# Which heads share an attention step, and on which half of the matmul array each score lands

## The reference, cut to what matters

```
# 8 query heads of 64, in 2 key groups of 4; a chunk is 64 tokens, the window is 2 chunks
scores = einsum('bnqhgd,bnkhd->bnhgqk', q, k) * 64 ** -0.5
scores = scores - slope[head] * |distance|           # ALiBi, one slope per head
probs  = softmax([scores, sink[head]])[..., :-1]      # one sink logit per head
out    = einsum('bnhgqk,bnkhd->bnqhgd', probs, v)     # heads of a group share k and v
```

## Time and profile before

| | |
|---|---|
| median of the runs | 683.0 us (682.1 to 683.81) |
| the profiled execution: its own time | 682.08 us |
| the profiled execution: span from first to last instruction | 680.4 us |
| PE busy | 652.1 us, 96% of the span |
| DVE busy | 477.3 us, 70% |
| ACT busy | 397.7 us, 58% |
| mean granted TensorE clock | 0.99 of full speed |
| PE's share of the chain that ended last | 86% |

### The profile page before, as it was taken

One profiled execution on the slowest core, in us unless ns is written; L12 is line 12 of the kernel. 1 busy time (PEld: TensorE's weight loads), 2 busy tenths in 40 slices (PEclk: granted clock), 3 DMA queues, 4 the chain that ended last, 5 costly groups with the idle time before them and its releaser, 6 DMA issues.

```text
span 680.4 us, 9400 instructions
## 1 busy us (share of the span) xinstructions
PE 652.1 (96%) x3421; PEld 543.7 (80%) x3421; DVE 477.3 (70%) x801; ACT 397.7 (58%) x675; POOL 170.6 (25%) x217
## 2 busy tenths in 40 slices
PE   5999999999999999999999998889999999999985
PEld 4788878788888888888888886778888888888763
DVE  5788995264632435424674637999999999998877
ACT  7448584255633332334452356277898889898853
POOL 7000008992000000000000000324647546556100
PEclk9999999999999999999999999789999999999999
DMA  8557534213222211111314904658687887885663
GB/s 267 183 154 203 126 99 134 63 62 79 67 63 64 63 63 62 63 63 63 123 63 159 395 26 164 223 171 260 217 272 214 298 268 237 297 254 181 230 266 124
DMA packets 75840, 108.51 MB, mean 159 GB/s; under 512 B 31767, under 2 KB 53344, under 8 KB 75666
## 3 DMA queue, kind: packets, MB, share of 16 engines
q1 hardware_dynamic: 63232, 99.76, 44.9%
q0 software_dynamic: 12448, 8.11, 4.0%
q10 hardware_dynamic: 114, 0.04, 0.0%
HBM read 123.90 MB, written 20.98 MB: 213 GB/s over the span
## 4 chain that ended last, share of the span: by engine, by line
PE 86%; DVE 8%; DMA 2%; ACT 2%; issue 1%; SPq 0%; POOLq 0%; DVEq 0%; ACTq 0%
PE bank L1714 22%; PE bank L1716 22%; PE bank L1715 22%; PE bank L2138 3%; PE bank L1866 2%; DMA expert_rows<-expert_rows_hbm 1%; PE bank L1772 1%; PE bank L2056 1%; PE bank L1885 1%; PE bank L1925 1%; PE bank L1935 1%; DVE rank_onehot L1550 1%; PE bank L1898 1%; PE bank L1721 1%; DVE gate_up_lo L1434 1%
## 5 line engine op out<-in xcount | busy, mean ns | idle before, releaser
L1714 PE MATMUL bank<-h_hi,w_hi 128*128 128x512 f32 x304 | 123.8, 407 | 1.3 <-DVE h_lo L1137 1.3
L1716 PE MATMUL bank<-h_hi,w_lo 128*128 128x512 f32 x304 | 118.8, 391 | 0.0
L1715 PE MATMUL bank<-h_lo,w_hi 128*128 128x512 f32 x304 | 118.5, 390 | 0.0
L1434 DVE TENSOR_TENSOR gate_up_lo<-ew_raw,gate_up_hi 128x1024 fp32r<-128x1024 f32 x92 | 108.4, 1219 | 5.2 <-ACT gate_up_hi L999 5.0
L728 POOL DMA_INDIRECT unit_tokens<-ffn_rows,row_index x23 | 29.2, 1271 | 277.7 <-DVE row_index L1558 266.1
L1115 DVE TENSOR_TENSOR w_lo<-w_raw,w_hi 128x2048 fp32r<-128x2048 f32 x26 | 59.8, 2299 | 48.6 <-ACT w_hi L790 48.5
L999 ACT ACTIVATE gate_up_hi<-ew_raw 128x1024 fp32r<-128x1024 f32 x92 | 91.9, 1052 | 0.0
L1714 PE MATMUL bank<-gate_up_hi,unit_in_hi 128*128 128x512 f32 x184 | 76.6, 416 | 0.3 <-DVE unit_in_lo L1585 0.3
L1716 PE MATMUL bank<-gate_up_hi,unit_in_lo 128*128 128x512 f32 x184 | 72.6, 395 | 0.0
L1715 PE MATMUL bank<-gate_up_lo,unit_in_hi 128*128 128x512 f32 x184 | 72.5, 394 | 0.0
L1714 PEld LDWEIGHTS bank<-h_hi,w_hi 128*128 128x128 f32 x304 | 57.2, 188 | 13.1 <-issue 2.3
(11 more groups left out here) (381 smaller groups left out, 1317.8 us busy)
## 6 DMA issues: line engine op xcount, KB each, us to landing
w_raw<-in_w_in SPq DMA_DIRECT2D x16, 1024.0 KB, 5.3
ew_raw<-in_w_gate SPq DMA_DIRECT2D x32, 512.0 KB
ew_raw<-in_w_up SPq DMA_DIRECT2D x32, 512.0 KB
ew_raw<-in_w_down SPq DMA_DIRECT2D x32, 512.0 KB
expert_rows_hbm<-sub_product SPq DMA_DIRECT2D x16, 256.0 KB
w_raw<-in_w_out SPq DMA_DIRECT2D x4, 1024.0 KB, 5.1
expert_rows<-expert_rows_hbm SPq DMA_DIRECT2D x8, 512.0 KB, 7.4
x_T<-in_x SPq DMA_DIRECT2D x4, 512.0 KB, 5.4
```

The source lines that it names most:

```text
L1434: dve.tensor_tensor(dst, eraw[slot][:, :], hi.bitcast(F32), ALU.subtract).then_inc(elo_done, 1)
L1714: pe.matmul(out_ap, lhs_hi, rhs_hi, start=first, stop=False)
L1715: pe.matmul(out_ap, lhs_hi, rhs_lo, start=False, stop=False)
L1716: return pe.matmul(out_ap, lhs_lo, rhs_hi, start=False, stop=last)
```

## The change

Parity of the step is now `part`, and step `part` of a tile takes two heads of each key group: heads 2·part and 2·part+1 of group 0 and of group 1. Place i of a step (0 to 3) holds head `head_of(part, i)`. The four score matmuls are issued in the order of places 0, 2, 1, 3: group 0, group 1, group 0, group 1, so rows 0 to 63, 64 to 127, 0 to 63, 64 to 127 of the array, and banks 0, 1, 0, 1. The rows of `alibi_bias` are stored by place, the sinks are read through a strided view of 2 by 2 elements, the value matmuls pick their column slice per place, and the final transposes pick the pair of places that holds heads 2k and 2k+1.

```
+        def head_of(part, i):
+            return i // 2, 2 * part + i % 2
+        def head_place(h):
+            g, j = divmod(h, GRP)
+            return GRP * (j // 2) + 2 * g + j % 2
...
-                        dve.scalar_tensor_tensor(bias[:, h, :], dist_m[:, :], -slope, wmask[:, :], ALU.mult, ALU.add)
+                        dve.scalar_tensor_tensor(bias[:, head_place(h), :], dist_m[:, :], -slope, wmask[:, :], ALU.mult, ALU.add)
...
-                g, c0, v = a_ % 2, CHUNK if a_ >= 2 else P, a_ % 2
-                heads = slice(GRP * g, GRP * (g + 1))
+                part, c0, v = a_ % 2, CHUNK if a_ >= 2 else P, a_ % 2
+                sink = sinkb[:, :].rearrange("p (g a j) -> p a g j", g=KVB, a=2)[:, part, :, :]
+                by_group = lambda tile: tile[:, :].rearrange("p (g j) -> p g j", g=KVB)
...
-                link(dve.tensor_tensor(mxs[v][:, :], mxs[v][:, :], sinkb[:, heads], ALU.max))
+                link(dve.tensor_tensor(by_group(mxs[v]), by_group(mxs[v]), sink, ALU.max))
...
-                dve.tensor_tensor(esk[v][:, :], sinkb[:, heads], mxs[v][:, :], ALU.subtract).then_inc(max_done, 1)
+                dve.tensor_tensor(by_group(esk[v]), sink, by_group(mxs[v]), ALU.subtract).then_inc(max_done, 1)
...
-                for h in range(GRP):
-                    o = ps[h // 2][:, 256 * (h % 2) + c0:256 * (h % 2) + 256]
-                    ins = pe.matmul(o, qb[d, h, m * P:(m + 1) * P], kb[d, m * P - P + c0:(m + 1) * P],
+                for i in (0, 2, 1, 3):
+                    g, j = head_of(part, i)
+                    d = slice(DB * g, DB * (g + 1))
+                    o = ps[i // 2][:, 256 * (i % 2) + c0:256 * (i % 2) + 256]
+                    ins = pe.matmul(o, qb[d, j, m * P:(m + 1) * P], kb[d, m * P - P + c0:(m + 1) * P],
                                     start=True, stop=True)
...
-                for h in range(GRP):
-                    o = ps[4][:, DB * h:DB * (h + 1)]
+                for i in range(GRP):
+                    g = head_of(part, i)[0]
+                    d = slice(DB * g, DB * (g + 1))
+                    o = ps[4][:, DB * i:DB * (i + 1)]
                     if m:
-                        pe.matmul(o, pt[:, 0, h, :], vb[:, m - 1, d], start=True, stop=False)
-                    ins = pe.matmul(o, pt[:, 1, h, :], vb[:, m, d], start=not m, stop=True)
+                        pe.matmul(o, pt[:, 0, i, :], vb[:, m - 1, d], start=True, stop=False)
+                    ins = pe.matmul(o, pt[:, 1, i, :], vb[:, m, d], start=not m, stop=True)
...
-                        ins = pe.transpose(bank4(5)[:, k, :], ob_t[:, 2 * k:2 * k + 2, :], ident[:, :])
+                        p0 = head_place(2 * k)
+                        ins = pe.transpose(bank4(5)[:, k, :], ob_t[:, p0:p0 + 2, :], ident[:, :])
```

More of the change, by code:

```diff
@@ L1285, in score_max @@
                     bank = ps[b][:, :].rearrange("p (h c) -> p h c", h=2)
-                    hs = GRP * g + 2 * b
+                    hs = GRP * part + 2 * b
                     ins = dve.scalar_tensor_tensor(pb[v][:, 2 * b:2 * b + 2, c0:], bank[:, :, c0:], DB ** -0.5,
@@ L1858, in scores @@
             def scores(a_):
-                m, g = a_ // 2, a_ % 2
-                d = slice(DB * g, DB * (g + 1))
+                m, part = a_ // 2, a_ % 2
                 c0 = CHUNK if m else P
@@ L1893, in _ @@
                     pe.wait_ge(ob_ready, a_)
-                for h in range(GRP):
-                    o = ps[4][:, DB * h:DB * (h + 1)]
+                for i in range(GRP):
+                    g = head_of(part, i)[0]
+                    d = slice(DB * g, DB * (g + 1))
+                    o = ps[4][:, DB * i:DB * (i + 1)]
                     if m:
-                        pe.matmul(o, pt[:, 0, h, :], vb[:, m - 1, d], start=True, stop=False)
-                    ins = pe.matmul(o, pt[:, 1, h, :], vb[:, m, d], start=not m, stop=True)
+                        pe.matmul(o, pt[:, 0, i, :], vb[:, m - 1, d], start=True, stop=False)
+                    ins = pe.matmul(o, pt[:, 1, i, :], vb[:, m, d], start=not m, stop=True)
                 ins.then_inc(pv_ps, 1)
                 side(1 if a_ < 6 else 0)
-                if g == 1:
+                if part == 1:
                     pe.wait_ge(ob_ready, a_ + 1)
```

## The result

The changed kernel takes 679.15 us (median of 7 runs, 676.41 to 680.06) against 682.79 us before (7 runs, 681.49 to 683.81). The ratio is 0.9945, with a 95% interval of 0.9930 to 0.9961: faster, by 3.6 us. Timed again later it was 0.9949 (0.9930 to 0.9968).

What follows compares the result with a forecast made beforehand. PE was taken to bound attention, with scores on its chain; 5 x 0.34 + 2 x 0.04 = 1.8 us saved, step 7 and the rest nothing, gave 683.0 - 1.8 = 681.2 us, range 679.2 to 685.6.

Steps and rivals of the forecast that it cites:

- What bounds: Attention stage: PE is busy 56.07 of 57.10 us, scores are on the chain, so PE savings reach the end.
- The scores: Score matmuls: halves overlap, weight loads stay serial at 0.105 us; gain 0.34 us per 192-key step, 0.04 with 128.
- The upper bound: Score matmuls: two records side by side at three changes of half, five spacings for eight; at most 3.1 us in all.
- The rival of full pairs: Score matmuls: loads of both halves overlap too, each change of half hides a record; 3.1 us less, 679.9 us, chance 0.21.
- Step 7: Last attention step: DVE splits a weight tile until 181.69 us, so shorter scores only lengthen PE's wait; pays nothing.
- Cover in steps 2 to 6: Attention: idle time on DVE (shortest 1.68 us) and ACT (0.71) exceeds 0.34 us, so the scores' gain comes through.
- their cost at nothing: Sixteen small DVE instructions reading sinks in two pairs: still four elements, so no added cost.
- No overlap: Score matmuls: the array takes records in turn whatever their rows; time stays 683.0 us, chance 0.18.
- a costly change of half: Inside each step's scores: three changes of half cost 0.20 us each, 4.8 us in all, 687.8 us; slower case's chance 0.19.

Runs made afterwards that it cites:

- half-by-half: Changed kernel with a step's score matmuls ordered lower, lower, upper, upper in place of lower, upper, lower, upper; 678.93 us, ratio 0.9937.
- the late split: Kernel before, with DVE's split of a weight tile moved behind the maxima of step 7; 683.16 us, ratio 1.0015.
- the banks alternated: Kernel before, with only the score matmuls' order changed so that PSUM banks alternate and the half of the rows does not; 682.27 us, ratio 1.0002.

## Where the prediction was right and where it failed

**What bounds.** Right. PE is the chain through attention, what the scores save comes forward in full, and the 225 us behind attention keep it to 0.1 us wherever the clock stays up. No transfer came late.

**The scores.** This is the step that failed: "matmuls of two halves overlap but weight loads remain one after another at 0.105 us". The loads of the two halves overlap too (two in 0.19 us), so a step of 192 keys gained 0.64 us in place of 0.34 and one of 128 keys 0.44 in place of 0.04. The row behind the assumption was read correctly, a spacing of 0.105 us that does not fall with the columns. But it came from matmuls that all stood on the same rows, the value matmuls on all 128 and the scores on one half; it says nothing on two loads into different halves. To call the serial load "the one thing that the trace shows" was to carry a row over to a case that it doesn't cover.

**The upper bound.** It failed as well. "At each of the three places two records run fully side by side, so a step lasts five spacings" takes the two records of a float32 matmul as a block that the other half has to wait for. The halves are more independent than that, a stretch lasts four spacings, and the bound should have been 5 x 0.65 + 2 x 0.45 = 4.2 us. The rival of full pairs, at 3.1 us, was right in kind and carried the same count; with it went the range's lower end, 679.2 against 679.15 us measured.

**Step 7.** Nearly right. PE's wait grew from 0.41 to 0.92 us, so of 0.64 us saved 0.13 arrived, not nothing: the 0.12 us that the split had to spare. Moving the split released 0.5 us of it in the changed kernel and none in the one before.

**Cover in steps 2 to 6.** Right for ACT and DVE's wait for the scores (1.12 us was the least left), but a wait was missed that the kernel before does not have in its profile: PE stands 0.34 us at the output transposes of step 1. DVE's two instructions that read the sinks in pairs did not grow as a whole, 203 and 286 ns in the mean against 259 and 276, so their cost at nothing held. DVE's small instructions in front of that output are drawn out while POOL works, in these two profiles at different ones. The three behind the maximum over keys, first the changed kernel and then the half-by-half one, on the same step:

```profile
151.03 0.45 DVE L1301 TENSOR_TENSOR score_max<-score_max,sinks_b 128x4 f32<-128x4 f32 x1
151.51 0.17 DVE L1302 TENSOR_SCALAR score_max_neg<-score_max 128x4 f32<-128x4 f32 x1
151.59 0.44 DVE L1303 TENSOR_TENSOR sink_term<-sinks_b,score_max 128x4 f32<-128x4 f32 x1
```

```profile
152.13 0.16 DVE L1301 TENSOR_TENSOR score_max<-score_max,sinks_b 128x4 f32<-128x4 f32 x1
152.32 0.33 DVE L1302 TENSOR_SCALAR score_max_neg<-score_max 128x4 f32<-128x4 f32 x1
152.57 0.15 DVE L1303 TENSOR_TENSOR sink_term<-sinks_b,score_max 128x4 f32<-128x4 f32 x1
```

1.06 against 0.64 us in sum. Where it is 1.06, PE waits 0.34 us; where it is 0.64, PE has no such wait. It changes between profiles of the very same kernel (51.73 and 52.05 us of attention). The old grouping has a smaller form of it as well: from the transposes of the probabilities to those of the output step 1 takes 3.52 us in the profile of before, but 3.69 with the late split and 3.75 with the banks alternated, against 3.96 here and 3.57 half by half. So I take it as no effect of the change, nor of its strided reads of the sinks: an undisturbed L1301 takes 0.16 us as before. The largest form, 0.34 us of idle time, was seen in the changed grouping only, in three of eleven profiles. That POOL is the disturber was not tested alone; the long ones stop with POOL's work, which ends at 160.2 us in the changed kernel; from 162 us on these three take 0.15 to 0.17 us.

**The sum, settled.** 5 x 0.64 + 2 x 0.44 + 0.13 - 0.34 = 3.87 us of attention by the parts, 3.78 measured; the 0.1 between them is in step 1, which is 3.96 - 3.52 = 0.44 us longer, not 0.34. The term that was mis-sized is the scores' 5 x 0.34 + 2 x 0.04 = 1.8 us, which measured 5 x 0.64 + 2 x 0.44 = 4.1. That the total came out as near as 3.6 us to the rival's 3.1 is partly the wait in step 1, which took some of it back.

**The rivals.** No overlap and a costly change of half are excluded by every run. The idle time on the loads of the scores is 2.1 us in eight places in the changed kernel as before, all of it where the shape changes from 128 to 64 rows, and none at a change of half. The Trainium skill, TensorEngine Tiling (Array Packing), Key Properties, says that a change of tiling mode drains the engine and a change of tile alone does not. The trace agrees with both parts. The order of starts is another matter. The Trainium skill, TensorE: Matmul & The Clock Gate, Part 3, The mechanism, has matmuls start and end strictly in program order. The half-by-half run contradicts this for the starts: an upper half that starts no sooner than the last lower record would be 0.27 + 2 x 0.162 = 0.59 us late, and the stretch lasts 0.93 us, not 1.5. The measurement decides; whether the ends keep the order was not tested.

## What to carry to other kernels

Before pricing an overlap, ask which of the rows that limit it were taken on the same resource: a serial spacing on the whole array bounds nothing on its halves. Matmuls of 64 rows whose operands lie in the two halves of the partitions should stand near each other in PE's stream, four or fewer float32 records of one half before the other's; a strict alternation is not needed. All that was measured here had the two halves write to different banks. And when a stage gets shorter, look at each engine's last instruction before it: a helper that had 0.12 us to spare becomes the next bound.

## What the runs showed of the hardware that was not expected

- Matmuls on rows 0 to 63 and on rows 64 to 127 run side by side, loads included: eight float32 records in 0.92 us in place of 1.56, sixteen in 1.57.
- One half overtakes waiting work of the other, but only past three waiting records: no delay behind four records, 0.43 us behind six, 0.76 us behind eight (with 192 keys).
- The array works through both halves at the full rate of each: the spacing within a half stays 0.162 us at 192 columns and 0.112 us at 128.
